# The rotation of attention's keys behind the substitution for the inverses, and two pairs of output sums at other rounds of it

## The reference

```python
u = _rms_norm(h, pre_mix_g[layer])
proj = jnp.einsum('btd,dp->btp', u, w_in[layer])
q, k, v, rw, gates = jnp.split(proj, IN_SPLITS, axis=-1)
...
q = _rope(q.reshape(B, T, 2 * H, dq), pos)          # x1*cos - x2*sin, x2*cos + x1*sin
k = _rope(k.reshape(B, T, 2 * H, dq), pos)
...
S = S * w_t[..., None, :] + sa[..., None] * b_t[..., None, :] + v_t[..., None] * k_t[..., None, :]
```

## Time and profile before

| what | value |
|---|---|
| median of 3 runs | 2877.91 us (2877.18 to 2881.73) |
| the profiled execution's own time | 2874.55 us |
| its span in the profile | 2872.8 us |
| PE busy with matmuls | 2695.8 us, 94% of the span |
| DVE busy | 1528.9 us, 53% |
| ACT busy | 1035.0 us, 36% |
| POOL busy | 840.8 us, 29% |
| mean granted TensorE clock | 0.973 of full speed |

### The profile page before, as it was taken

One profiled execution on the slowest core, in us unless ns is written; L12 is line 12 of the kernel. 1 busy time (PEld: TensorE's weight loads), 2 busy tenths in 40 slices (PEclk: granted clock), 3 DMA queues, 4 the chain that ended last, 5 costly groups with the idle time before them and its releaser, 6 DMA issues. The chain is left out here.

```text
span 2872.8 us, 47220 instructions
## 1 busy us (share of the span) xinstructions
PE 2695.8 (94%) x18992; PEld 1883.0 (66%) x18992; DVE 1528.9 (53%) x2575; ACT 1035.0 (36%) x1955; POOL 840.8 (29%) x569
## 2 busy tenths in 40 slices
PE   8889898989899998899999999979999999999999
PEld 6677786868677777788887777754444444444443
DVE  3677676767676767477775555554421111112513
ACT  3324243433433333466676677653300000000001
POOL 1454444435272625100000134341243333320000
PEclk9998999999999999999999999989999999999999
DMA  3142424334242424244410676864311111113012
GB/s 98 61 167 87 143 101 156 133 119 147 97 154 82 169 83 167 71 111 102 122 35 22 159 181 159 187 207 129 131 44 44 44 44 44 44 44 132 0 37 88
DMA packets 192519, 297.88 MB, mean 104 GB/s; under 512 B 84480, under 2 KB 119072, under 8 KB 186032
## 3 DMA queue, kind: packets, MB, share of 16 engines
q1 hardware_dynamic: 184240, 260.72, 30.2%
q10 hardware_dynamic: 8064, 34.15, 2.9%
HBM read 188.54 MB, written 106.27 MB: 103 GB/s over the span
## 5 line engine op out<-in xcount | busy, mean ns | idle before, releaser
L684 PE MATMUL pp_ps<-uT,pp_w 128*128 128x260 f32 x1536 | 349.8, 383 | 0.0
L684 PEld LDWEIGHTS pp_ps<-uT,pp_w 128*128 128x128 f32 x1536 | 288.7, 189 | 49.7 <-issue 1.2
L684 PE MATMUL pp_ps<-pp_t,pp_s 128*128 128x260 f32 x1024 | 245.1, 400 | 22.3 <-DVE pp_raw L1290 21.8
L684 PEld LDWEIGHTS pp_ps<-pp_t,pp_s 128*128 128x128 f32 x1024 | 204.1, 200 | 59.3 <-issue 24.7
L1909 DVE TENSOR_SCALAR_CACHE_REDUCE at_p<-at_S 128x1040 f32<-128x1040 f32 x128 | 153.7, 1239 | 68.4 <-PE at_S L1747 68.4
L684 PE MATMUL pp_ps<-uT,pp_s 128*128 128x260 f32 x512 | 136.9, 427 | 48.3 <-DVE pp_raw L1280 48.3
L1852 ACT ACTIVATE at_p<-at_p,at_mn 128x1040 f32<-128x1040 f32 x128 | 148.7, 1163 | 47.4 <-DVE at_p L1909 47.2
L2768 PE MATMUL fh_b<-u2T,fh_ws 128*128 128x512 f32 x352 | 158.2, 592 | 0.0
L684 PEld LDWEIGHTS pp_ps<-uT,pp_s 128*128 128x128 f32 x512 | 108.7, 215 | 73.5 <-issue 53.6
L2768 PE MATMUL fh_b<-fh_t,fh_ws 128*128 128x512 f32 x352 | 154.7, 592 | 0.0
L1747 PE MATMUL at_S<-at_kR,at_qR 64*128 64x512 f32 (+1 forms) x768 | 144.0, 498 | 10.6 <-DVE at_p L1909 6.0
(11 more groups left out here) (339 smaller groups left out, 5296.7 us busy)
## 6 DMA issues: line engine op xcount, KB each, us to landing
pp_w<-in_w_main SPq DMA_DIRECT2D x64, 512.0 KB, 4.6
fh_w<-in_w_ffn_in SPq DMA_DIRECT2D x44, 512.0 KB, 4.4
rc_kb<-s_kb SPq DMA_DIRECT2D x64, 256.0 KB, 4.2
rc_aw<-s_ar SPq DMA_DIRECT2D x64, 256.0 KB, 4.2
s_ar<-pp_ar SPq DMA_DIRECT2D x8, 1088.0 KB, 4.0
s_kb<-pp_kb SPq DMA_DIRECT2D x8, 1088.0 KB, 6.2
s_vz<-pp_vz SPq DMA_DIRECT2D x8, 1088.0 KB, 12.8
s_x<-pp_xa ACTq DMA_DIRECT2D x8, 1056.0 KB, 3.9
```

Source lines behind the costliest of these rows:

```text
L684: ins = nc.tensor.matmul(out, weights[:, k, :], moving[:, k, :], start=(start and k == 0), stop=(k == KH_IN - 1), skip_group_check=True)
```

## The change

Four edits, all in the projection loop:

- DVE: `keep_c22` of the pair `following(i)` stands behind round 10 of the substitution instead of round 12, `keep_c12` behind round 18 instead of round 26.
- POOL: before it rotates the keys of head i, it waits for `solved` of head i.
- SP: `return_solved(i)` stands at the end of head i, ahead of the store of the keys, instead of in the next head.
- SP: the store of the keys stands behind it, so that SP's wait for the rotation does not hold back the way of the inverses. In the last head the loads for attention's first head stand ahead of both.

```diff
@@ sync @@
                 for i in range(HEADS):
-                    if i >= 2:
-                        return_solved(i - 1)
                     if i != 1:
                         load_pair(nth(0, i) + 2)
-                    if i == 1:
-                        return_solved(0)
                     load_pair(nth(1, i) + 2)
...
                     sp.dma_start(kept_d[KEPT.index("att_q"), i], home("att_q")).then_inc(stored[0], 16)
                     load_pair(nth(*following(i)) + 2)
-                    sp.wait_ge(rope_summed, 2 * i + 2)
-                    sp.dma_start(kept_d[KEPT.index("att_k"), i], home("att_k")).then_inc(stored[1], 16)
                     if i == HEADS - 1:
...
                         first_head.load(sp, kept_d, lambdas)
-                return_solved(HEADS - 1)
+                    return_solved(i)
+                    sp.wait_ge(rope_summed, 2 * i + 2)
+                    sp.dma_start(kept_d[KEPT.index("att_k"), i], home("att_k")).then_inc(stored[1], 16)
@@ gpsimd @@
                     sum_weights(q + 1)
+                    after(pool, "solved", i)
                     rope("att_k", i)
@@ vector @@
-                    eliminate(i, range(0, 12))
+                    eliminate(i, range(0, 10))
                     keep_c22(q, 1)
                     keep_c22(q, 0)
-                    eliminate(i, range(12, 26))
+                    eliminate(i, range(10, 18))
                     keep_c12(q, 1)
                     keep_c12(q, 0)
-                    eliminate(i, range(26, HB - 2))
+                    eliminate(i, range(18, HB - 2))
```

## The result

| | kernel before | changed kernel |
|---|---|---|
| median | 2879.82 us (4 runs, 2877.18 to 2887.26) | 2782.28 us (4 runs, 2781.76 to 2793.65) |
| profiled execution's own time | 2874.55 us | 2781.76 us |
| its span | 2872.8 us | 2779.8 us |
| mean granted TensorE clock | 0.973 | 0.984 |

The changed kernel takes 0.9667 of the time (95% interval 0.9636 to 0.9698), some 97 us less. The prediction named 2780.5 us.

A forecast was written before the change was run, and what follows sets the result against it. PE is busy 94% of the span, so only its idle or slow-clock time can be won: 85.8 (heads 1 to 6) + 12 (head 7) - 0.4 = 97.4 us, giving a median of 2780.5 us; range 2768 to 2822.

The forecast's parts named there:

- POOL holds DVE step by step: Substitution: POOL's SBUF reads block DVE instruction by instruction; a 0.38 us step took 2.55, as long as POOL's running instruction.
- `keep_c22` behind round 10: Head 2, DVE: second sum done at 451.65, about 453.9 if blocked twice; PE's 6.41 us wait goes.
- Rounds 10 to 17 and `keep_c12`: Head 2, DVE: rounds end at 459.4, `keep_c12` at 460.15, PE wants it at 461.3; the 3.54 us wait goes.
- `solved` 33 us after the first round: Sign in DVE's substitution: `solved` comes 33 us after the first round instead of 41.
- The rotation, 7.8 us: POOL, head 2: keys' rotation from 468.6 to 476.4, weight sum done at 477.7, needed at 479.0; slack 1.3 us.
- The transposition beside the weight sum: DVE's 1.24 us transposition falls near POOL's weight sum; cost between 0 and 1.24 us, taken as 0.
- SP not on the path: SP's store, weight load and inverses' way back cost nothing: inverses back by 477.9, PE asks after 482.
- Heads 1 to 7: PE's idle and slow time goes: 85.8 us in heads 1 to 6; head 7 gains 12 of 15.0.
- Head 0 to head 1: The 13.0 us wait before line 787 shrinks but wins nothing, as `mix` needs POOL's neighbours; +0.4 us.
- POOL not the cause: Rival: DMA or something else slows rounds 8 to 11; gain 6.2 us per head, 2838 us; chance 0.08.
- A residue: Rival: slack at `keep_c12` or weight sum is used up; 7 to 42 us return, 2788 to 2822; chance 0.23.
- Half cancelled by a DVE chain bound to the weights: Rival: a later DVE chain in the loop starts with the weights, not PE; half the gain, 2830; chance 0.05.

The follow-up runs named there:

- e4: Kernel before, with POOL rotating only 8 of 1040 columns of the keys, other columns left unrotated; 2833.30 us, ratio 0.9857.
- e1: Kernel before, with only the output sums moved to rounds 10 and 18, POOL and SP as before; 2838.74 us, ratio 0.9881.
- e6: Changed kernel with six useless multiplications (4.80 us) on POOL between its wait for `solved` and the keys' rotation; 2800.58 us, ratio 0.9747.
- e3: Changed kernel with SP in its old order, the keys' store ahead of the inverses' way back; 2842.81 us, ratio 0.9888.
- r1: The changed kernel run again, unaltered, on another chip; 2781.17 us, ratio 0.9681 to the kernel before there.
- e7: Changed kernel with POOL making the neighbours of head 1's k ahead of its wait for `solved` of head 0; 2780.53 us, ratio 0.9680.
- r4: Changed kernel with head 1's neighbours first, last `join` behind product 4, head 0's keys rotated after DVE's `kd_1` of head 1; 2764.53 us, ratio 0.9624.

## Why the prediction was right

*POOL holds DVE step by step: right, and e4 shows it.* One reading of the prediction was loose: a held step is not exactly as long as POOL's instruction. The one at 440.55 ends at 443.10, 0.2 us behind POOL's, which ends at 442.87.

*`keep_c22` behind round 10: right.* Taken at 451.65 on the old time scale, with 0.74 us and no blocking. It took 0.74 us at 433.85, beside POOL's instruction of 433.81, which ran 1.43 us. The upper end (both halves blocked) did not happen.

*Rounds 10 to 17 and `keep_c12`: right, slack 1.4 us instead of 1.1.* They took 7.4 us (434.52 to 441.95), against the 10 that would have spoken against me. Two-partition steps are 0.19 us. e1 shows the other side: with the keys beside them, these rounds take so long that `keep_c12` is 5.85 us late.

*`solved` 33 us after the first round: right.* It is 32.6 (418.44 to 451.00).

*The rotation, 7.8 us: too long.* It took 7.2 (451.17 to 458.36), since the old row was measured with DVE in its way (two of its three instructions took 2.63, now all take 2.38 or 2.39). Slack at the weight sum therefore 2.0 us, not 1.3. e6 measures 2.2.

*The transposition beside the weight sum, taken at 0: right.* The two met exactly, both at 458.32, and took 1.25 and 1.27 us, as alone. The rule of the Trainium skill that I had set beside it (SBUF — State Buffer, the practical consequences) holds in this row. On that page it holds only outside DVE's 2-port modes. I had left that condition out, and it matters for `TENSOR_SCALAR`, below.

*SP not on the path: right in this order,* and e3 shows what the order is worth: 61 us.

*Heads 1 to 7.* Up to the start of the last `join` the changed kernel has gained 1162.87 - 1062.56 = 100.3 us, after a wait of 2.4 there. The patterns thus gave 102.7 us, where I had 85.8 + 15.0 = 100.8. The idle time agrees (66.5 us less, where the rows of the pattern give 66.7); PE's busy time between these two places fell by 36.2 us, where the rows give 34.2, and that is the difference. At `join` I had 2 us of wait and up to 1 of lower clock; it was 2.4 and none in that execution. In r1, the same kernel, it was 1.80 us and the product behind it took 5.41 us instead of 3.77, with a granted clock of 0.50 from 1062.9 to 1066.3, where the first profile of the changed kernel has 1.00. In e7, alike at this place, it was 2.38 and 3.0. So the term is 2.4 to 5.4 us, and I was lucky with this one.

*Head 0 to head 1: 0.0 instead of +0.4.* Head 1's first product starts at 235.60, before at 235.56. That the 13.0 us would turn into a wait at the start of head 1, behind POOL's neighbours, was right. That DVE's `TENSOR_SCALAR` at line 1402 would be blocked too (2.88 us against 0.76), and `mix` behind it (2.28 against 1.30), I had not seen; it did not matter there, since `mix` waited for the neighbours anyway.

*Behind the loop: a term I did not have.* The forecast took those stages as unchanged. They took 1693.8 us before and 1701.1 after. In the twelve other profiled executions they took 1694.3 to 1702.8 us, and the two executions of the same changed kernel 1701.1 and 1699.4. I see no edit that it follows: e4 (1694.3) and r4 (1696.1) are short, e3 (1702.8) is long. The profile of before was simply the shortest of the fourteen, and 5.4 of the 7.3 us are PE's busy time, so mostly its clock; why it differs stays open. So in the profiles the gain is 100.3 - 7.3 = 93.0 us of span, in the medians 97.5, and the closeness of 2780.5 to 2782.28 is partly luck, errors of opposite sign: 2.9 us of gain too little in the loop, 7.3 too much behind it, and the 3.4 us that I added from the profiled execution to a median, which were 0.5 in the changed kernel.

*The rivals.* POOL not the cause: refuted by e4. A residue: not in the changed kernel; e6 shows what it looks like, from 2 us of delay on. Half cancelled by a DVE chain bound to the weights: nothing of it, PE waits for no engine longer than 0.5 us in heads 2 to 6. Slower: e3, which has the change without its SP part, is the nearest that I found, and is still 30 us faster than before. The 3 us that I had given the loop before it decides were 2.0 to 2.2.

## What to carry to other kernels

Where DVE and POOL both work from SBUF, look in the timeline for short DVE steps that last until POOL's running instruction ends, and give POOL's long instructions a place beside DVE steps that were seen not to be held (here a transposition, a reciprocal and output sums that read PSUM), not beside a chain of short ones with two inputs. A wait on POOL that does this makes a loop with what stands behind it; work out that loop's slack, and move whatever queue (here SP) would carry the new wait over to a third party. A part can look useless or harmful without the one that it needs: the sums and the wait gave 30 us with SP in its old order, and about 90 with the new one.

## What the runs showed of the hardware

- A DVE step with two SBUF inputs (two tiles, or two parts of one) that meets a running instruction of POOL's rotation waits for its end whatever its own size: 2.35 to 2.55 us instead of 0.2 to 0.4. Sums with one input in PSUM (0.74), the transposition (1.25) and the reciprocal (6.61) were not held.
- A `TENSOR_SCALAR` with one input in SBUF was held nevertheless: 2.88 instead of 0.76 us on 1040 columns, 2.35 instead of 0.17 on 16. The Trainium skill (SBUF — State Buffer, Who interferes with whom) says that this operation can enter a mode in which it takes the pair of ports shared with POOL; the row fits that, with 0.76 us for 1040 columns where a step with two inputs takes 1.24. I had thought of two-input steps alone. Where such a step began first, it was not held: in e7 one on 1024 columns starts at 223.20 and takes 0.68 us, and POOL's weight sum at 223.22 takes 1.79 instead of 1.27.
- So the one that starts first goes on, and POOL is held in return when it is DVE. In the kernel before, a DVE step of 0.35 us began at 445.33, and POOL's instruction at 445.42 took 2.52 us instead of 2.38. In e7, beside that chain, two instructions of the rotation took 2.83 and 3.25 us, in head 2 of the changed kernel 2.39 and 2.38 with DVE elsewhere.
- What the clock costs behind a short gap can't be read from its length. Behind 2.42 us (changed kernel) nothing was lost, behind 2.38 (e7) 3.0 us in two groups, behind 1.80 (r1) 1.6; behind six gaps of 2.56 to 2.60 us in e6 only the first cost more than 0.1 us (5.46 us for 16 matmuls, the others 3.77 to 3.78). In the kernel before it was 0.1 behind 3.54 us and 3.0 behind 3.11. A forecast for one such gap needs both values.
- Within the 128 small matmuls of `join` PE sometimes pauses for 0.6 to 1.4 us with no releaser in the profile (`[1.16 <-issue]` above). Wherever it comes, it comes with 3 matmuls left in head 1, 15 in head 2 and 27 in head 3, before the change too; in e3 and e6 it is absent. Slow matmuls can follow: in the changed kernel's head 2 the 12 low-rank products behind it took 3.15 us instead of 2.02. What it is stays open.
